# One encoder layer in float32r passes on one core: the last stages put into one block, half of w_gate split beside the output projection, and the queue of the last two head pairs reordered

## The reference, cut to what matters

```python
qkv  = x @ w_qkv                                   # 1024 x 3072
mix  = neighbourhood_attention(qkv, rpb) @ w_o     # window 8 x 16, bias, softmax
x1   = layer_norm(ALPHA * x + mix, ln1_g, ln1_b)   # ALPHA = 2 ** 0.25
hid  = square(relu(x1 @ w_ff1))                    # 1024 x 4096
ple  = sigmoid(x1 @ w_gate) * (p @ w_proj)         # p: 1024 x 256
out  = layer_norm(ALPHA * x1 + hid @ w_ff2 + ple, ln2_g, ln2_b)
```

## Time and profile before

| | us |
|---|---|
| median of 3 runs | 1269.86 (1268.87 to 1269.94) |
| the profiled execution | 1270.37 |
| its span | 1268.5 |
| TensorE busy in the span | 1231.6 (97%) |
| VectorE / ScalarE / GpSimd busy | 857.3 / 577.7 / 119.2 |

### The profile page before, as it was taken

One profiled execution on the slowest core, in us unless ns is written; L12 is line 12 of the kernel. 1 busy time (PEld: TensorE's weight loads), 2 busy tenths in 40 slices (PEclk: granted clock), 3 DMA queues, 4 the chain that ended last, 5 costly groups with the idle time before them and its releaser, 6 DMA issues.

```text
span 1268.5 us, 17717 instructions
## 1 busy us (share of the span) xinstructions
PE 1231.6 (97%) x5864; PEld 1032.2 (81%) x5864; DVE 857.3 (68%) x1707; ACT 577.7 (46%) x1108; POOL 119.2 (9%) x78
## 2 busy tenths in 40 slices
PE   7999999999999699989999999999999999999997
PEld 6888888888887578868888888888888888888886
DVE  4477677777777447766777667667665475588786
ACT  4355555655656642122335444444444433333671
POOL 0211221221122423100000000000000000000000
PEclk9999999999999899989999999999999999999999
DMA  8423223223223736454535444434459778668533
GB/s 195 94 60 83 56 71 86 53 71 88 53 71 111 233 116 177 134 185 152 175 125 176 146 142 168 147 142 168 148 197 350 251 277 305 218 222 311 200 115 100
DMA packets 139342, 195.75 MB, mean 154 GB/s; under 512 B 10496, under 2 KB 72832, under 8 KB 139264
## 3 DMA queue, kind: packets, MB, share of 16 engines
q1 hardware_dynamic: 139264, 194.80, 48.0%
HBM read 136.04 MB, written 50.52 MB: 147 GB/s over the span
## 4 chain that ended last, share of the span: by engine, by line
PE 54%; DVE 1%; ACT 0%; issue 0%; DVEq 0%; ACTq 0%
PE bank L2394 24%; PE bank L2362 23%; PE bank L2322 7%; DVE weight_parts L1959 0%; ACT weight_parts L1756 0%; DVE hidden_staging L2107 0%; DVE y L2300 0%; DVE weight_raw L1978 0%; DVE y L2307 0%; DVE ln_stats L196 0%; DVE hidden_staging L2075 0%; DVE y L2195 0%; DVE weight_sum L1978 0%; DVE weight_parts L1941 0%; DVE hidden_staging L2077 0%
## 5 line engine op out<-in xcount | busy, mean ns | idle before, releaser
L714 ACT ACTIVATE probabilities<-negated_scores,negated_max 128x384 f32<-128x384 f32 (+1 forms) x128 | 75.5, 590 | 141.3 <-DVE negated_max L919 141.0
L1036 PE MATMUL bank<-act_T_hi,w_qkv_hi 128*128 128x512 f32 x336 | 133.6, 398 | 0.0
L1036 PE MATMUL bank<-act_T_lo,w_qkv_hi 128*128 128x512 f32 x336 | 133.6, 398 | 0.0
L1036 PE MATMUL bank<-act_T_hi,w_qkv_lo 128*128 128x512 f32 x336 | 131.9, 393 | 0.0
L900 DVE TENSOR_TENSOR prob_T_lo<-bank,prob_T_hi 128x256 fp32r<-128x256 f32 (+2 forms) x160 | 69.0, 448 | 79.4 <-ACT prob_T_hi L705 77.9
L2362 PE MATMUL bank<-x_combination,weight_parts 128*128 128x512 f32 x480 | 112.8, 389 | 0.0
L2362 PEld LDWEIGHTS bank<-x_combination,weight_parts 128*128 128x128 f32 x480 | 90.0, 188 | 19.1 <-DVE hidden_staging L2107 0.5
L2322 PE MATMUL bank<-weight_parts,act_T_hi 128*128 128x512 f32 x256 | 80.8, 397 | 3.1 <-DVE weight_parts L1941 3.1
L596 POOL TENSOR_TENSOR w_qkv_lo<-weight_raw,w_qkv_hi 128x1024 fp32r<-128x1024 f32 x21 | 50.3, 2396 | 267.2 <-ACT w_qkv_hi L659 267.2
L2394 PE MATMUL bank<-weight_parts,weight_parts_early 128*128 128x512 f32 x312 | 73.0, 389 | 0.0
L2394 PE MATMUL bank<-weight_parts 128*128 128x512 f32 x312 | 73.0, 389 | 0.0
(11 more groups left out here) (245 smaller groups left out, 2821.8 us busy)
## 6 DMA issues: line engine op xcount, KB each, us to landing
hidden_combinations<-hidden_staging SPq DMA_DIRECT2D x112, 256.0 KB, 2.0
w_ff_in<-in_w_ff SPq DMA_DIRECT2D x27, 1024.0 KB, 7.8
weight_raw<-in_w_ff SPq DMA_DIRECT2D x25, 1024.0 KB, 5.6
weight_raw<-hidden_combinations SPq DMA_DIRECT2D x14, 1024.0 KB, 5.4
hidden_in<-hidden_combinations SPq DMA_DIRECT2D x14, 1024.0 KB, 5.6
weight_raw<-in_na_w_qkv SPq DMA_DIRECT2D x24, 512.0 KB, 4.4
bias_in<-rpb_rows SPq DMA_DIRECT2D x256, 6.0 KB
attention_T<-out_T SPq DMA_DIRECT2D x8, 512.0 KB, 2.9
```

The costliest lines, as they stand in the source:

```text
L714: nc.scalar.activation(prob[:, u % 4, 0:n], score[:, u % 2, 0:n], ACT.Exp, scale=-1.0, bias=nmax[:, u % 4:u % 4 + 1], accum_out=total[:, u ...
L1036: mm = nc.tensor.matmul(proj_ps[gi % 2][:, :], w[wp][:, (par + kind) % 2, k, :], S.act[ap][:, k, t * HALF:(t + 1) * HALF], start=(i == 0), ...
```

## The change

All stages are put into one `nc.Block()`. TensorE makes gate tile 0 before it transposes the last tile of x1. The first half of w_gate is loaded, copied (ScalarE) and subtracted (GpSimd) inside the output projection, in tiles 2, 3, 5 and 7. The tiles of the gate's second half, the places of some buffers, and the loads of the last two pairs are moved accordingly. The gate's accumulators move from banks 6 and 7 to banks 0 and 1. The diff, cut to its core:

```diff
-WO_SPLIT_STEP = (3, 4, 5, 7, 8, 9, 16, 17)
-WO_LOAD_STEP = {5: 4, 6: 5, 8: 6, 9: 7}
+WO_SPLIT_STEP = (1, 2, 4, 5, 7, 8, 16, 17)
+WO_LOAD_STEP = {4: 4, 5: 5, 7: 6, 8: 7}
-EARLY_LOAD_STEP = 2
+EARLY_LOAD_STEP = (2, 3)
+LN_LOAD_STEP = (11, 13)
+GATE_LOAD_TILE = (1, 1, 4, 5)
+GATE_SPLIT_TILE = (2, 3, 5)
...
+def gate_high(nc, act, S, half, i):
+    slot = i if half else 2 + i % 2
+    act.wait_ge(S.ff_in[slot], 16 * (1 + i // 2) if not half else 16 if slot < 2 else 48)
+    nc.scalar.activation(S.gate_w[0][i][:, :], gate_raw(S, half, i), ACT.Copy).then_inc(S.gate_hi, 1)
+def gate_low(nc, eng, engine_of, S, half, i):
+    eng.wait_ge(S.gate_hi, 4 * half + i + 1)
+    engine_of.tensor_tensor(S.gate_w[1][i][:, :], gate_raw(S, half, i), S.gate_w[0][i][:, :].bitcast(F32),
+                            ALU.subtract).then_inc(S.gate_lo, 1)
...
 # SP, last pair: the four first w_o loads are no longer at its head, but in pair 6,
 # ahead of the store of pair 6; ln1 gain and shift at u = 11 and 13, not at 0
-                    for n in range(4):
-                        ...
-                        load_rows(sp, S, n, w_o, n * P).then_inc(S.wo_in[n], 16)
+                        if u in LN_LOAD_STEP:
+                            ...
+                if more and not loads:
+                    for n in range(4):
+                        if n < PC:
+                            sp.wait_ge(proj_w_lo, n + 1)
+                        else:
+                            sp.wait_ge(p_turned, 2 * (n - 1))
+                        load_rows(sp, S, n, w_o, n * P).then_inc(S.wo_in[n], 16)
...
 # SP, output projection
                     load_attention(2, 0)
+                    sp.wait_ge(o_lo, 2 + 2)
                     load_x(1, 1)
...
+                for i in range(BLOCK_CHUNKS):
+                    if GATE_LOAD_TILE[i] == t:
+                        if i < 2:
+                            sp.wait_ge(wo_lo, KC - 1 + i)
+                        else:
+                            sp.wait_ge(S.gate_lo, i - 1)
+                        load_gate(sp, S, w_gate, 0, i)
...
 # GpSimd, tile(t), after the lower part of attention tile t
+                if t in GATE_SPLIT_TILE:
+                    gate_low(nc, pool, nc.gpsimd, S, 0, GATE_SPLIT_TILE.index(t))
+                if t == GROUPS - 1:
+                    gate_low(nc, pool, nc.gpsimd, S, 0, 3)
...
 # ScalarE
             def tile(t, par, nth):
                 if t < GROUPS - 2:
                     split(t + 2, par, nth + 1)
+                if t in GATE_SPLIT_TILE:
+                    i = GATE_SPLIT_TILE.index(t)
+                    ...
+                    gate_high(nc, act, S, 0, i)
+                if t == GROUPS - 1:
+                    act.wait_ge(y_full, 2 * t + (2 + 4))
+                    gate_high(nc, act, S, 0, 3)
+                    x1_high(nc, act, S, t - 1)
                 act.wait_ge(chain, LN_STEPS * t + 4)
                 nc.scalar.activation(mv[:, par, 3:4], mv[:, par, 2:3], ACT.Sqrt).then_inc(deviation, 1)
-                if t:
-                    turned_x1(t - 1, 1 - par)
-                if t == GROUPS - 1:
-                    turned_x1(t, par)
+                if 0 < t < GROUPS - 1:
+                    x1_high(nc, act, S, t - 1)
...
 # TensorE: turn_x1(GROUPS - 1) leaves tile(7) and comes behind gate tile 0
             for u in range(GATE_TILES):
                 gate(u)
+                if u == 0:
+                    turn_x1(nc, pe, S, GROUPS - 1)
...
 # SP, start of the gate
+            sp.wait_ge(S.y_free, 2 * GROUPS + 4)
+            for u in range(3):
+                ...
+                load_gate_tile(u)
+            for i in range(2):
+                load_gate(sp, S, w_gate, 1, i)
+            store_x1(sp, S, GROUPS - 1)
...
 # combinations of x1 beside the gate: u = 1 to 6 instead of 0 to 5
-            if u in (GROUPS - 2, GROUPS - 1) or u >= GATE_TILES - 2:
+            if u in (0, GROUPS - 1) or u >= GATE_TILES - 2:
                 return None
-            return divmod(u if u < GROUPS else u - 2, 3)
+            return divmod(u - 1 if u < GROUPS else u - 2, 3)
-            return {3: 0, 6: 1, 11: 2, 14: 3}.get(u)
+            return {4: 0, 7: 1, 11: 2, 14: 3}.get(u)
...
 # VectorE, gate
+                if u == 0:
+                    x1_low(nc, dve, S, GROUPS - 1)
+                    dve.wait_ge(S.x1_lo, 2 * GROUPS + 4)
+                    for i in range(2):
+                        dve.wait_ge(S.x1_stored[i], 16 * (GROUPS // 2 + 1))
```

More of the change, by code:

```diff
@@ L126, in build_program @@
         S.free_at = aligned(nc.sbuf_base)
+        KB = 1024
+        S.x1_tile = nc.alloc_sbuf_tensor_at("x1_tile", [P, 2, D], F32, offset=S.free_at + 96 * KB)
+        S.gate_w = [[nc.alloc_sbuf_tensor_at(f"gate_w_{n}{i}", [P, D], F32R, offset=S.free_at + place * KB)
+                     for i, place in enumerate(places)]
+                    for n, places in (("hi", (76, 84, 64, 68)), ("lo", (80, 88, 92, 72)))]
         S.ps = [ctx.enter_context(nc.psum_tensor(f"bank{i}", [P, HALF], F32)) for i in range(8)]
@@ L184, in load_gate, with gate_raw, x1_T_tile, turn_x1 @@
 def load_gate(sp, S, w_gate, half, i):
-    load_rows(sp, S, i, w_gate, 2 * i * P, 2, HALF, half * HALF).then_inc(S.ff_in[i], 16)
+    slot = i if half else 2 + i % 2
+    load_rows(sp, S, slot, w_gate, 2 * i * P, 2, HALF, half * HALF).then_inc(S.ff_in[slot], 16)
+def gate_raw(S, half, i):
+    return S.raw[:, i if half else 2 + i % 2, :]
+def gate_high(nc, act, S, half, i):
+    slot = i if half else 2 + i % 2
+    act.wait_ge(S.ff_in[slot], 16 * (1 + i // 2) if not half else 16 if slot < 2 else 48)
[4 more added lines that the diff above has]
+                            ALU.subtract).then_inc(S.gate_lo, 1)
+def x1_T_tile(S, t, q):
+    return S.ps[4 + 2 * (t % 2) + q]
+def turn_x1(nc, pe, S, t):
+    for q in range(2):
+        pe.wait_ge(S.x1_ready, 2 * t + (q + 1))
+        pe.wait_ge(S.x1_lo, 2 * t + (q + 1))
+        for i in range(4):
+            k = 4 * q + i
+            mm = nc.tensor.transpose(x1_T_tile(S, t, q)[:, i * P:(i + 1) * P],
+                                     S.x1_tile[:, t % 2, k * P:(k + 1) * P], S.ident[:, :])
+        mm.then_inc(S.x1_turned, 1)
+def x1_high(nc, act, S, t):
+    for q in range(2):
+        act.wait_ge(S.x1_turned, 2 * t + (q + 1))
+        nc.scalar.activation(S.act[0][:, 4 * q:4 * q + 4, t * P:(t + 1) * P],
+                             x1_T_tile(S, t, q)[:, :].rearrange("p (i t) -> p i t", i=4), ACT.Copy).then_inc(S.x1_hi, 1)
+def x1_low(nc, dve, S, t):
+    for q in range(2):
+        dve.wait_ge(S.x1_hi, 2 * t + (q + 1))
+        nc.vector.tensor_tensor(S.act[1][:, 4 * q:4 * q + 4, t * P:(t + 1) * P],
+                                x1_T_tile(S, t, q)[:, :].rearrange("p (i t) -> p i t", i=4),
+                                S.act[0][:, 4 * q:4 * q + 4, t * P:(t + 1) * P].bitcast(F32),
+                                ALU.subtract).then_inc(S.x1_lo, 1)
+def store_x1(sp, S, t):
+    sp.wait_ge(S.x1_ready, 2 * t + 2)
+    sp.dma_start(S.x1[t], S.x1_tile[:, t % 2, :]).then_inc(S.x1_stored[t % 2], 16)
 def broadcast_row(a):
@@ L1007, in tile @@
                 if t:
[L1008 to L1017, removed]
+                    x1_low(nc, dve, S, t - 1)
             for each in TILES:
@@ L1242, in _ @@
             early_products(1, 6, 2 * KC)
[L1244 to L1252, removed]
             def tile(t, par, nth):
@@ L1565, in load_w1 @@
                 if u < 2:
-                    sp.wait_ge(w_lo, chunks(6 + 2 * u))
+                    sp.wait_ge(w_lo, 6 + 2 * u)
                 else:
@@ L1720, in gate_sigmoid @@
                     act.wait_ge(gate_step, 2 * (u - 1))
-                nc.scalar.activation(gated[u % 2], S.ps[6 + u % 2][:, :], ACT.Sigmoid).then_inc(sigmoid, 1)
+                nc.scalar.activation(gated[u % 2], S.ps[u % 2][:, :], ACT.Sigmoid).then_inc(sigmoid, 1)
             def x_high(j):
@@ L2078, in _ @@
                                                op0=ALU.mult, op1=ALU.add).then_inc(gate_step, 1)
+                if u == 0:
+                    x1_low(nc, dve, S, GROUPS - 1)
+                    dve.wait_ge(S.x1_lo, 2 * GROUPS + 4)
+                    for i in range(2):
+                        dve.wait_ge(S.x1_stored[i], 16 * (GROUPS // 2 + 1))
                 if u == GROUPS - 1:
-                    low(7)
+                    gate_low(nc, dve, nc.vector, S, 1, 3)
                 if x_ends(u) is not None:
@@ L2091, in _ @@
                 if u == GROUPS - 2:
-                    for m in range(4, 7):
-                        low(m)
+                    for i in range(3):
+                        gate_low(nc, dve, nc.vector, S, 1, i)
                 if u == GATE_TILES - 2:
@@ L2336, in unit_product @@
                         pe.wait_ge(relu_done, in_units(u - 1, A11))
+                    else:
+                        pe.wait_ge(sigmoid, GATE_TILES - 1 + u)
                 elif p == 2:
```

133 lines of the change are left out of this document (46 added, 87 removed).

## The result

The changed kernel takes 1279.68 us (median of 4 runs, 1278.12 to 1280.8) against 1269.90 for the kernel before on the same chip (4 runs, 1268.87 to 1270.38): a ratio of 1.0077, 95% interval 1.006 to 1.0095, so 9.8 us slower. The forecast was 1280.0. The profiled execution has a span of 1278.0 us, 9.5 more than before.

A forecast was written before the change was run, and what follows sets the result against it. PE, busy 1231.6 of 1268.5 us, was taken as the bound, so only its idle or slow time could be won. -10.5 - 9.2 + 22.7 + 6.9 = +9.9 on 1270.4, less 0.5, gave about 1280 us, range 1271 to 1287.

The forecast's parts named there:

- A, last pairs: Last pairs: reordered loads let the first `embedded` store land early, removing ACT's 10.89 us wait; -10.5 us, bounds -11.5 and -8.
- B, boundary: Output projection to gate: TensorE's two 3.1 us waits and the half clock go; -9.2 us, bounds -10.1 and -7.5.
- C, three stalls: Output projection: POOL's queue order delays tiles 3, 4, 6; 19.7 us bare plus VectorE delays, +22.7, bounds 19.7 and 25.
- C, clock: PE at half clock after each of the three stalls: 3 x 2.3, +6.9 us, bounds 0 and 7.8.
- C in all: Output projection: the three stalls from POOL's queue plus the half clock after them, +29.6 us.
- the wait for `v_T`: Sign in PE's waits, last pairs: falls from 12.5 us to 2 or less.
- its recorded rival: Load order alone, last pairs: the 2.2 us half clock after the long wait adds to the gain, up to -12.5 us.
- gate tile 8: In the gate: VectorE's added combination steps make lower parts late, so TensorE waits about 0.7 us.
- R1: Faster: POOL's queue doesn't hold TensorE in the output projection, leaving A + B = -19.7, 1250 us; 6 in 100.
- R2: No change: output projection stalls come bare, without clock loss or VectorE delay; 1270 us; 5 in 100.
- R3: Slower still: stores stay the bound in the last pair, half or all of A lost; 1285 to 1290; 9 in 100.
- R4: The boundary doesn't close, tile 7's x1 or w_gate's second half being late; B is -5, 1284 us; 5 in 100.

The follow-up runs named there:

- experiment 3: Kernel before with only the change's new order of loads and w_o copies in the last two pairs: 1259.11 us, ratio 0.9914.
- experiment 4: Changed kernel with GpSimd's gate_low one tile later and the old order of loads and w_o copies: 1260.49 us, ratio 0.9925 to the kernel before.
- experiment 1: Changed kernel with GpSimd's gate_low(0), (1), (2) one tile later in its queue, behind the attention tile's lower part: 1250.52 us, ratio 0.9848 to the kernel before.
- experiment 5: Changed kernel with 30 matmuls of unread result added on TensorE before each of its three waits: 1273.14 us, ratio 1.0028 to the kernel before.
- experiment 6: Changed kernel, VectorE waiting for GpSimd's lower part of tile t+1 before finishing the layer norm of tiles 2, 3 and 5: 1276.12 us.
- experiments 7 and 8: Kernel before with only the ln1 loads moved to u = 11 and 13 (7: 1266.49 us), or only four w_o loads ahead of pair 6's store (8: 1264.36 us).

## Why the prediction was right

It was right in the time, and nearly so term by term:

| step | predicted | measured | by |
|---|---|---|---|
| A, last pairs | -10.5 | -10.65 | experiment 3 |
| B, boundary | -9.2 | -9.27 | experiment 4 |
| C, three stalls | +22.7 | +22.6 | starts of tiles 3, 4, 6 against experiment 1 |
| C, clock | +6.9 | +6.5 | experiment 5 |
| C in all | +29.6 | +29.2 | against experiment 1 |
| sum | +9.9 | +9.8 | the result |

The measured A, B and C in all add up to +9.2 and not to +9.8, since the two gains come to -19.2 together where they give -19.9 one by one. The forecast has no such term. That its sum lies within 0.1 us is luck in part: against these 0.7 us stand A, B and C, each 0.1 to 0.4 us above what was measured, 0.7 in all.

**A.** ACT no longer waits for `ple_embedding`, and its two exponentials are 10.9 us closer. One sign was given wrongly: the wait for `v_T` was to fall to 2 us or less and fell to 3.4. The 12.5 us of the earlier trace rows were one wait of 9.2 and six short ones, 3.3 together; the sum used only ACT's long wait, and the short ones were never part of what the loads cause. They are the same in experiments 1 and 3. The half clock behind the long wait, 2.2 us by the earlier trace rows, was rightly left out of A: the gain of experiment 3, 10.65 us, is no more than what ACT gained, and the 12.5 of its recorded rival did not come.

**B.** This is the piece of the chain of waits in the changed kernel (start, us, what):

```profile
569.77 0.87 PE bank L236 x8
570.64 5.49 PE bank L2360 x24
...
577.01 32.67 PE bank L2360 x144
...
619.48 39.75 PE bank L2360 x174
```

A tile of 24 gate matmuls takes 5.49 us. From the start of tile 6's transposes (569.61) to the gate's end (659.23) it is 89.6 us; 89.7 was forecast, 98.9 was before. At gate tile 8 the wait was 0.3 us and not 0.7; the tiles behind the first took 5.46 us on average and not 5.44, which makes up for it. The 0.2 us added for tile 7's layer norm has no run of its own.

**C, the stalls.** They came before tiles 3, 4 and 6, none before 5 and 7. The forecast was of how much later these tiles start: 7.5, 7.6 and 7.6 us. They start 7.71, 7.46 and 7.46 us later than in experiment 1. Its two parts were both a little off, in opposite directions. Bare, they are 19.2 us (experiment 6, counted the same way: 6.72, 6.24 and 6.24) and not 19.7: two subtractions alone take 4.63 us from start to end and not 4.80, three times. VectorE's share is 3.4 and not 3.0, and lies otherwise than forecast: 1.0 at tile 3 and 1.2 at each of the others, where 0.6 and 1.2 were set.

**C, the clock.** 3 x 2.3 from two windows of half clock in the kernel before held: three windows of 3.6 to 4.9 us at 0.50, worth 6.4 us by their halves and 6.5 by experiment 5. The size was scaled from two windows; that it would be the same after waits of 7 us was a guess between cases of 3 and 9 us, and it came true.

**The rivals.** R1 and R2 fell with the three waits and the clock of 0.50 behind them; R1's time, 1250, is just what experiment 1 reaches (1250.52), but by another way than R1 gives: the upper part of w_gate is as late as before, and only the lower part of tile 3 no longer stands behind it. R3 fell with ACT's wait, and R4 with the gate's end. R3 was not groundless: with only one of the two loads moved (experiments 7 and 8) the stores stay the bound, at 7.21 and 4.86 us.

## What to carry to other kernels

An instruction that is free on an idle engine is not free in its queue: ask what its input waits for, and what stands behind it. If the producer of its input is itself queued behind a wait for the bottleneck engine's current tile, then everything behind it is as late as that, and moving it one step down the queue can cost nothing (here it gave 29 us). Count a stall of TensorE of a few microseconds with the half clock that follows it, here 6.5 us on 22.6.

## What was unexpected of the hardware

Filling a stall with matmuls whose result nobody reads is worth time: three stalls of about 7 us, filled with 30 matmuls each, left the clock at 1.00 and the kernel 6.5 us faster, and the stalls themselves grew by only 0.1 us each. And the loads did not quite cost by their bytes: 1 MB of ln1 loads was worth 3.4 us and 2 MB of w_o loads 5.5 us, against 10.65 for the whole new order.
